# Square of a finished token tile ahead of the Relu, and a last down job that is summed cell by cell

## The reference, cut to what matters

```python
h = rmsnorm(x, lw['n2_pre']) * (1.0 + sc2) + sh2
u = jnp.square(jax.nn.relu(h @ lw['w_up'])) @ lw['w_down']     # hidden width 4096
x = x + gt2 * rmsnorm(u, lw['n2_post'])
```

## Time and profile before

| | |
|---|---|
| median of three runs | 2001.87 us (2001.72 to 2005.58) |
| the profiled execution | 2002.41 us |
| its span on the core | 2000.7 us |
| instructions | 36043 |
| mean granted clock of TensorE | 0.98 |

### The profile page before, as it was taken

The page is one execution under the profiler, slowest core; times in us unless marked ns, Lnnn a source line. Parts: engine busy times, 40 slices in busy tenths (PEclk is TensorE's granted clock), DMA queues, the critical chain, the costliest instruction groups (busy, mean ns, idle before and its releaser), DMA issues.

```text
span 2000.7 us, 36043 instructions
## 1 busy us (share of the span) xinstructions
PE 1873.4 (94%) x13992; PEld 1651.5 (83%) x13992; DVE 1020.7 (51%) x1679; ACT 772.5 (39%) x1335; POOL 242.5 (12%) x384
## 2 busy tenths in 40 slices
PE   4989989788999999999999999999999989999996
PEld 2767868655888888777777778999999989999996
DVE  2644253445444544111111455676777857686967
ACT  5544453423324332101011333645455445545453
POOL 2221020213201111101110043000000010000001
PEclk9999999879999999999999999999999999999998
DMA  8011011288310221422232343333333343333333
GB/s 291 25 41 44 23 34 40 71 278 304 87 53 23 64 53 35 147 74 85 86 102 81 109 134 105 86 106 85 106 85 97 90 112 98 106 85 103 88 85 93
DMA packets 221701, 190.89 MB, mean 95 GB/s; under 512 B 11753, under 2 KB 195354, under 8 KB 220538
## 3 DMA queue, kind: packets, MB, share of 16 engines
q1 hardware_dynamic: 202704, 135.88, 23.4%
q0 software_dynamic: 16832, 50.48, 8.7%
q10 hardware_dynamic: 2026, 2.59, 0.4%
HBM read 173.00 MB, written 15.91 MB: 94 GB/s over the span
## 4 chain that ended last, share of the span: by engine, by line
PE 83%; DVE 4%; ACT 3%; issue 3%; DMA 2%; POOL 1%; POOLq 1%; SPq 1%; ACTq 1%; PEld 1%; DVEq 0%; PEldq 0%
PE psum L280 24%; PE psum L2458 19%; PE psum L2469 17%; PE psum L2339 6%; PE psum L2385 4%; PE psum L2077 2%; PE psum L2090 1%; DVE nmax L1514 1%; ACT work L1110 1%; PE psum L2158 1%; DMA work<-in_cache_k 1%; PE psum L2313 1%; PE psum L2152 1%; DMA work<-in_cache_v 1%; PE psum L2259 1%
## 5 line engine op out<-in xcount | busy, mean ns | idle before, releaser
L2458 PE MATMUL psum<-h_hi,region_r 128*128 128x272 f32 x2048 | 344.7, 289 | 0.0
L2469 PE MATMUL psum<-region_r 128*128 128x272 f32 x2688 | 342.6, 289 | 2.1 <-DVE region L1909 1.6
L2469 PEld LDWEIGHTS psum<-region_r 128*128 128x128 f32 x2688 | 338.9, 188 | 5.0 <-DVE region_r L1827 2.4
L1827 DVE TENSOR_TENSOR region_r<-region,region_r 128x512 fp32r<-128x512 f32 x352 | 242.5, 692 | 147.5 <-ACT region_r L1264 146.1
L2458 PEld LDWEIGHTS psum<-h_hi,region_r 128*128 128x128 f32 x2048 | 292.2, 189 | 0.3 <-DVE region_r L1827 0.2
L1264 ACT ACTIVATE region_r<-region 128x512 fp32r<-128x512 f32 x352 | 220.3, 628 | 167.9 <-PE psum L2469 143.9
L280 PE MATMUL psum<-h_hi,w_hi 128*128 128x288 f32 (+1 forms) x1056 | 239.4, 335 | 1.9 <-issue 1.1
L280 PE MATMUL psum<-h_lo,w_hi 128*128 128x288 f32 (+1 forms) x1056 | 233.2, 329 | 0.0
L280 PE MATMUL psum<-h_hi,w_lo 128*128 128x288 f32 (+1 forms) x1056 | 233.1, 329 | 0.0
L2458 PE MATMUL psum<-h_lo,region_r 128*128 128x272 f32 x1024 | 212.4, 289 | 0.0
L280 PEld LDWEIGHTS psum<-h_hi,w_hi 128*128 128x128 f32 x1056 | 159.4, 188 | 26.4 <-issue 10.2
(11 more groups left out here) (371 smaller groups left out, 2461.1 us busy)
## 6 DMA issues: line engine op xcount, KB each, us to landing
region<-in_w_mlp_up SPq DMA_DIRECT2D x64, 512.0 KB, 5.4
region<-in_w_mlp_down SPq DMA_DIRECT2D x64, 512.0 KB, 5.1
w_raw<-in_w_in SPq DMA_DIRECT2D x44, 512.0 KB, 3.9
work<-in_cache_k SPq DMA_DIRECT2D x64, 256.0 KB, 6.0
work<-in_cache_v POOLq DMA_DIRECT2D x64, 256.0 KB, 5.1
work<-in_ada_w POOLq DMA_DIRECT2D x32, 512.0 KB, 4.3
work<-in_ada_w SPq DMA_DIRECT2D x8, 1024.0 KB, 16.1
out<-work POOLq DMA_DIRECT2D x12, 512.0 KB, 4.0
```

The costliest lines, as they stand in the source:

```text
L1827: v.tensor_sub(ring_lo[n % RING], weight_of(n), ring_hi[n % RING].bitcast(F32)).then_inc(mw_lo, 1)
L2458: last = mm(outs[half], w[n % RING][:, k, :], m[:, 4 * part + k, at:at + H], start=(part == 0 and k == 0 and w is ring_hi and m is h_hi), ...
L2469: done = mm(job_bank(FIRST_BANK[q] + i), w[n % RING][:, k, :], m[k][:, at, :], start=(k == 0 and w is ring_hi and m is high), stop=(k == 3 ...
```

## The change

ScalarE's `fin_squares(0, f)` moves in its slot from behind `relu_out` and `square` to ahead of them. In the last down job VectorE adds cell by cell into yT, in the order C11, C12, C22, C21, instead of all at once; `y_added` reaches 32 with C12 and C22 in place, and 33 after C21. The end's tile order becomes 2, 3, 0, 1, 4, since tiles 2 and 3 need only C12 and C22; the bank pairs of the end become 6, 0, 4, 2, 6 (LATE works out to 0, 4, 2). The third tile of the end and `sample_columns(1)` wait for 33. `fin_tile` signals `fin_scaled` from the instruction itself, without a drain, and the last two tiles wait for that signal before the residual is added.

```diff
-        FIN_BANK = [[6, 6, 6, 6, 6], [6, 4, 2, 0, 6]]
+        LAST_BANKS = [(4, 5, 2, 3, 0, 1)[(FIRST[NQ] - 1 - back) % 6] for back in range(6)]
+        LATE = sorted((0, 2, 4), key=lambda at: -min(LAST_BANKS.index(at), LAST_BANKS.index(at + 1)))
+        FIN_BANK = [[6, 6, 6, 6, 6], [6, LATE[0], LATE[1], LATE[2], 6]]
...
+        def fin_tile_at(g, f):
+            return f if g == 0 else (2, 3, 0, 1, 4)[f]
...
             def sample_columns(g):
-                pool.wait_ge(y_added, 4 * NHB * (g + 1))
+                pool.wait_ge(y_added, 4 * NHB * (g + 1) + g)
...
             (ScalarE)
+                if n - 1 in FIN_AT:
+                    fin_squares(0, FIN_AT.index(n - 1))
                 if up and i % 2 == 1:
                     relu_out(q, i // 2)
...
-                if n - 1 in FIN_AT:
-                    fin_squares(0, FIN_AT.index(n - 1))
                 if n + RING < len(PRODUCTS):
                     weight_high(n + RING)
...
             (VectorE, output)
                 if i == 4:
                     v.tensor_add(cells[:, C21, :], u2, job_bank(n + 4)).then_inc(dve_read, 1)
+                    if q == NQ - 1:
+                        dve.wait_ge(dve_read, 8 * d + 2)
+                        v.tensor_add(yT[:, p, C11, :], yT[:, p, C11, :], cells[:, C11, :])
                 if i == 5:
...
+                    if q == NQ - 1:
+                        dve.wait_ge(dve_read, 8 * d + 5)
+                        v.tensor_add(yT[:, p, C12, :], yT[:, p, C12, :], cells[:, C12, :])
+                        dve.wait_ge(dve_read, 8 * d + 6)
+                        v.tensor_add(yT[:, p, C22, :], yT[:, p, C22, :], cells[:, C22, :]).then_inc(y_added, 1)
                 if i == 6:
                     v.tensor_add(out[:, C21, :], cells[:, C21, :], job_bank(n + 6)).then_inc(dve_read, 1)
+                    if q == NQ - 1:
+                        dve.wait_ge(dve_read, 8 * d + 7)
+                        v.tensor_add(yT[:, p, C21, :], yT[:, p, C21, :], cells[:, C21, :]).then_inc(y_added, 1)
+                        return
...
             (VectorE, fin_tile and the end)
                 v.scalar_tensor_tensor(fin_tok[g][f], fin_psum(g, f), stat[0:r, f:f + 1],
-                                       (post2_p if f < 4 else post2_s)[g], ALU.mult, ALU.mult)
-                dve.drain().then_inc(fin_scaled, 1)
+                                       (post2_p if f < 4 else post2_s)[g], ALU.mult, ALU.mult).then_inc(fin_scaled, 1)
...
                 if f >= 3:
+                    dve.wait_ge(fin_scaled, NF + f + 1)
                     dve.wait_ge(x_landed[3], 32 + 32)
...
             (TensorE, fin_transposed)
+                if g == 1 and f == 2:
+                    pe.wait_ge(y_added, 4 * NHB * 2 + 1)
...
-                        yT[:, c % 4, CELL[c // 4, f // 2], P * (f % 2):P * (f % 2) + P]
+                        yT[:, c % 4, CELL[c // 4, t // 2], P * (t % 2):P * (t % 2) + P]
```

More of the change, by code:

```diff
@@ L716, in rows_out @@
             def rows_out(g, f):
-                return yp_v[:, 4 * g + f, :] if f < 4 else ys_v[2 * HS * g:2 * HS * (g + 1), :]
+                return yp_v[:, 4 * g + fin_tile_at(g, f), :] if f < 4 else ys_v[2 * HS * g:2 * HS * (g + 1), :]
             for i in range(3):
@@ L978, in fin_store @@
                 pool.wait_ge(fin_scaled, NF * g + f + 1)
-                dst = yp_v[:, 4 * g + f, :] if f < 4 else ys_v[2 * HS * g:2 * HS * (g + 1), :]
+                dst = yp_v[:, 4 * g + fin_tile_at(g, f), :] if f < 4 else ys_v[2 * HS * g:2 * HS * (g + 1), :]
                 pool.dma_start(dst, fin_tok[g][f], accum_op=ALU.add)\
@@ L2488, in fin_transposed @@
             def fin_transposed(g, f):
-                at = 512 * FIN_BANK[g][f]
+                at, t = 512 * FIN_BANK[g][f], fin_tile_at(g, f)
                 if f == 0:
                     pe.wait_ge(y_added, 4 * NHB * (g + 1))
+                if g == 1 and f == 2:
+                    pe.wait_ge(y_added, 4 * NHB * 2 + 1)
                 if g == 0 and f > 0:
```

## The result

The changed kernel took 1982.01 us (median of five runs, 1978.26 to 1985.85). The kernel before, timed beside it, took 2001.72 us (five runs, 1996.21 to 2005.58). The ratio is 0.9906, with a 95% interval of 0.9882 to 0.9931, so 14 to 24 us of gain. Forecast were 1989.2 us and a range of 1988.0 to 1992.0: direction right, time and range missed, the gain larger than forecast.

A forecast was written before the change was run, and what follows sets the result against it. TensorE, busy 94% of the span, was taken as the bound. Gains of 10.8 us (Square moved) and 1.9 us (end) sum to 12.7, taking profiled execution from 2002.41 to 1989.7 us, median 1989.2; range 1988.0 to 1992.0.

The forecast's parts named there:

- Steps of 6.88 us: Finished tiles: without waits, each tile's transposes start 6.88 us after those of the tile before.
- in the middle: First to fifth finished tile's transposes: moving the Square saves 10.92 us less 0.1, so 10.8; bounds 8.5 and 11.
- at the end: Last down job onward: cell-by-cell additions start the transposes 1.85 us earlier; 1.9 us gained in all, bounds 1.0 and 2.1.
- additions in pairs: Last down job: the C12 and C22 additions follow 0.35 us apart and end beside product 351.
- the third scaling chain: Third tile's Square through scaling: frees the banks at 13.65 us, fourth transposes due at 13.76; 0.1 us of slack.
- The collision: Third tile's chain: GpSimd's small operation meets a 0.69 us VectorE subtraction; new wait taken as 0.1 us, bounds 0 and 0.6.
- The slower rival: ScalarE, held ahead of its Relu by late transposes, lets the weight ring run dry: 2006.6 us, chance 0.03.
- It stood 0.54 us above the median of three: Conversion to measured time: profiled execution 2002.41 us goes to 1989.7, and 0.54 us lower for the median, 1989.2.
- the bounds of the two gains: Square move gains 8.5 to 11 us, the end 1.0 to 2.1 us.
- one fall of the clock: Behind the longest wait, 2.75 us, the clock read 0.80; its recovery counts 1.63 us of the gain.
- the rows of the norm: Rival: broadcast norm rows loaded by SP hold VectorE's scaling, so the waits stay; 1999.9 to 2000.0 us, chance 0.05.
- the slack of the first tile: First finished tile: chain 2.2 us ahead of need, less 0.26 us lost to GpSimd's gather of sample columns.

The follow-up runs named there:

- b_shift16: Kernel before with sixteen more transposes of the identity after product 100, which moves the later waits in time; ratio 1.001 to the kernel before.
- a filled wait: Kernel before with sixteen transposes of the identity put into the longest wait, ahead of the fourth tile's transposes; ratio 0.9999 to the kernel before.

## Why the prediction was wrong

**Right: the mechanism and its size.** Steps of 6.88 us (forecast 6.88), 10.91 us in the middle (10.8), 1.94 and 0.21 at the end (1.9), additions in pairs 0.35 us apart, the third scaling chain 0.1 us ahead of need. In the profile of the changed kernel GpSimd's small operation there took 0.38 us instead of 0.22, beside a VectorE subtraction of two SBUF operands, and no wait of TensorE came of it, where 0.1 us had been allowed for. The collision that the rule of the Trainium skill on the shared port ("SBUF — State Buffer", "Who interferes with whom") gave is thus there. The slower rival did not come: where the Square was late in ScalarE's queue, the Relu stood at 1623.35, 4.35 after the transposes, and TensorE had no wait.

**Wrong: from the difference to the time.** The step that failed stands in the sum: "It stood 0.54 us above the median of three; of the median that makes 1989.2 us", together with a range of 4 us. It took everything outside the change to repeat itself, and put the spread of the runs at nothing: the bounds of the two gains alone, 9.5 and 13.1 us, already give 1988.8 to 1992.4. The runs showed that the kernel before spreads over 1989 to 2013 us, and that this goes with how long its clock stands at the lower level in its first 800 us, that its three shown runs were high draws (median 2001.87 where 88 later runs have 1997.8), and that the changed kernel's profile reached the changed code 8.93 us early in the same way. 1997.8 less 13 would have been 1985; measured were 1982.0 and 1982.4. The granted clock stood on the page of the kernel before, in fortieths of the span, with an 8 and a 7 between 350 and 450 us:

```profile
PEclk9999999879999999999999999999999999999998
```

A clock that falls so far upstream of the change was a reason to ask for the spread. The 93 runs of the kernel before have a standard deviation of 4.6 us, more than the whole width of the range.

**Wrong in a smaller way: one fall of the clock.** I counted the clock once, behind the longest wait, as the one profile had it. In `b_shift16` it falls behind three waits, 2.2 us more for the change. All runs together (93 of the kernel before, mean 1998.3; 11 of the changed one, mean 1982.7) give 15.6 us, with a standard error of 1.1: 2.5 more than the 13.1 of the profiles, and a little over two standard errors. More falls in the mean could give most of that, and part may be chance; how often each number of falls occurs was not measured, so this stays open.

**Half seen: the rows of the norm.** The prediction dismissed them with "GpSimd's result ended each of VectorE's idle times here". That was true only while ScalarE was late. With that link shortened, the DMA was last, and the slack of the first tile was 1.0 us and not 1.9 (2.2 less the 0.26 of the gather).

## What to carry to other kernels

Predict a difference from one profile, but take the absolute time and its range from the spread of runs; if TensorE's clock is below full anywhere upstream, the same program arrives at the changed code at different times. When one link of a chain is shortened, list what else the last instruction waits for, DMAs too: their slack was hidden by the link. Put an operation that frees another engine's buffer ahead of work that only refills a deep ring.

## What was not expected of the hardware

Waits of TensorE of 1.92 to 1.94 us, 7 us of work apart, cost nothing of the clock in one execution; in another the granted clock read 0.76 to 0.80 over the next 7 to 9 us. Behind a filled wait it stayed at 1.00. The step behind a fall was 1.5 us longer (10.56 against 9.02). "TensorE: Matmul & The Clock Gate", section "Why this matters for your kernels", of the Trainium skill warns of gaps longer than these, and longer than the 2.75 us that the prediction set beside it; here gaps under 2 us did it already.
